# Index scores rectified in place in PSUM and begun four steps sooner, low weights of a joint computed inside the pipeline of heads, two waits made finer

## The reference

```python
s = einsum('bqhd,bkd->bqhk', qib, ki)                 # 8 index heads of width 32, one shared key
score = einsum('bqhk,bqh->bqk', relu(s), wb)           # rectified, weighted, summed over heads
score = where(causal, score, -inf); _, sel = top_k(score, 128)
c_sel = c[sel]; logits = einsum('bqhd,bqkd->bqhk', qb, c_sel) * ATTN_SCALE
p = softmax(logits); out = einsum('bqhk,bqkd->bqhd', p, c_sel)
m = g0 * y_a + g1 * (out @ w_b) + g2 * y_c;  h = h + m @ w_o      # then a gated FFN
```

## Time and profile before

| | |
|---|---|
| median of three runs | 2055.36 us |
| the profiled execution: own time / span of the profile | 2055.58 us / 2053.4 us |
| PE matmuls busy | 2026.3 us, 99% of the span, 9561 records |
| PE weight loads busy (beside the matmuls) | 1675.5 us, 82% |
| DVE / ACT / POOL busy | 892.2 us (43%) / 720.7 us (35%) / 1020.1 us (50%) |
| chain that ended last | PE 94%, DVE 3%, POOL, ACT and issue 1% each |
| DMA | 188.20 MB, mean 92 GB/s |

### The profile page before, as it was taken

One profiled execution on the slowest core, in us unless ns is written; L12 is line 12 of the kernel. 1 busy time (PEld: TensorE's weight loads), 2 busy tenths in 40 slices (PEclk: granted clock), 3 DMA queues, 4 the chain that ended last, 5 costly groups with the idle time before them and its releaser, 6 DMA issues.

```text
span 2053.4 us, 26660 instructions
## 1 busy us (share of the span) xinstructions
PE 2026.3 (99%) x9561; PEld 1675.5 (82%) x9561; DVE 892.2 (43%) x1366; ACT 720.7 (35%) x990; POOL 1020.1 (50%) x783
## 2 busy tenths in 40 slices
PE   8999999999999999999999999999999999999999
PEld 7798887678888888888888887888877888888887
DVE  6778644534333322153334103568854533332124
ACT  6413224434322223232222223567543422222232
POOL 5345442135555554555555444666644555554543
PEclk9999999999999999999999999999999999999999
DMA  4232322013333332333333232332222333332232
GB/s 159 63 107 83 103 83 81 21 65 99 103 102 85 99 97 93 97 102 95 88 102 97 92 97 83 94 107 58 90 65 86 99 102 102 86 98 98 92 108 82
DMA packets 254152, 188.20 MB, mean 92 GB/s; under 512 B 7552, under 2 KB 249728, under 8 KB 254080
## 3 DMA queue, kind: packets, MB, share of 16 engines
q1 hardware_dynamic: 253392, 186.93, 30.4%
q10 hardware_dynamic: 688, 0.31, 0.1%
HBM read 180.93 MB, written 2.10 MB: 89 GB/s over the span
## 4 chain that ended last, share of the span: by engine, by line
PE 94%; DVE 3%; POOL 1%; issue 1%; ACT 1%; DMA 0%; SPq 0%; DVEq 0%; ACTq 0%; POOLq 0%
PE ps L600 29%; PE ps L602 29%; PE ps L601 28%; DVE sc L1430 1%; PE ps L823 1%; PE ps L808 1%; PE ps L966 1%; PE ps L889 1%; PE ps L891 1%; PE ps L890 1%; DVE ssum L1558 0%; POOL wlo L552 0%; PE ps L822 0%; PE ps L954 0%; PE ps L816 0%
## 5 line engine op out<-in xcount | busy, mean ns | idle before, releaser
L497 POOL TENSOR_TENSOR wlo<-raw,whi 128x512 fp32r<-128x512 f32 (+1 forms) x640 | 871.0, 1392 | 913.4 <-ACT whi L1030 913.1
L600 PE MATMUL ps<-xh,whi 128*128 128x512 f32 (+2 forms) x1912 | 732.9, 383 | 8.9 <-DVE xl L1430 7.4
L602 PE MATMUL ps<-xh,wlo 128*128 128x512 f32 (+2 forms) x1912 | 722.5, 378 | 0.0
L601 PE MATMUL ps<-xl,whi 128*128 128x512 f32 (+2 forms) x1912 | 722.2, 378 | 0.0
L1030 ACT ACTIVATE whi<-raw 128x2048 fp32r<-128x2048 f32 (+1 forms) x159 | 297.5, 1871 | 796.1 <-PE ps L602 792.9
L600 PEld LDWEIGHTS ps<-xh,whi 128*128 128x128 f32 (+1 forms) x1912 | 358.4, 187 | 77.5 <-issue 9.8
L602 PEld LDWEIGHTS ps<-xh,wlo 128*128 128x128 f32 (+1 forms) x1912 | 358.1, 187 | 68.0
L601 PEld LDWEIGHTS ps<-xl,whi 128*128 128x128 f32 (+1 forms) x1912 | 358.7, 188 | 64.9 <-issue 2.5
L1484 DVE TENSOR_TENSOR tmp<-ps,rs 128x512 f32<-128x512 f32 x148 | 102.1, 692 | 325.9 <-PE ps L602 308.6
L600 PE MATMUL ps<-fh,whi 128*128 128x512 f32 x528 | 205.4, 389 | 0.0
L602 PE MATMUL ps<-fh,wlo 128*128 128x512 f32 x528 | 205.4, 389 | 0.0
(11 more groups left out here) (290 smaller groups left out, 2208.1 us busy)
## 6 DMA issues: line engine op xcount, KB each, us to landing
raw<-in_w_in SPq DMA_DIRECT2D x90, 512.0 KB, 4.6
raw<-in_w_gate_up SPq DMA_DIRECT2D x44, 512.0 KB, 4.7
raw<-in_ffn_w_gate SPq DMA_DIRECT2D x44, 512.0 KB, 3.9
raw<-in_ffn_w_up SPq DMA_DIRECT2D x44, 512.0 KB, 5.1
raw<-in_ffn_w_down SPq DMA_DIRECT2D x32, 512.0 KB, 4.0
raw<-in_w_down SPq DMA_DIRECT2D x16, 512.0 KB, 3.9
raw<-in_ffn_w_down SPq DMA_DIRECT2D x16, 384.0 KB, 3.5
raw<-in_w_b SPq DMA_DIRECT2D x8, 512.0 KB, 3.9
```

Source lines behind the costliest of these rows:

```text
L497: ins = pool.tensor_tensor(wlo[:, c % 2, cs], raw[:, c % 2, cs], whi[:, c % 2, cs].bitcast(F32), ALU.subtract)
L600: pe.matmul(o, w_of(whi), xhi, start=first, stop=False)
L601: pe.matmul(o, w_of(whi), xlo, start=False, stop=False)
L602: return pe.matmul(o, w_of(wlo), xhi, start=False, stop=last)
```

## The change

1. **Scores.** ACT rectifies a score in place in its PSUM bank; DVE accumulates from PSUM; the SBUF buffers `rl` are gone. A bank is free again only after the accumulation (`score_acc` in place of `relu_done`). Score 0 moves from step (1, 0) to step (0, 4) of `C_Q+1`; `score_window` gives DVE's share per tile.
2. **Stack.** ACT writes `qst` and `kst` rows once (four copies and one); SP copies them to the repeated rows with two DMAs (32 partitions each: 66 KB for `kst`, 512 KB for `qst`), placed before the load of chunk `C_Q+3`. PE's first score waits for these copies.
3. **ACT's high weights** of `C_Q+3` and `C_U` are done in quarters between the rectifications.
4. **DVE.** The eight search steps among the scores go (the search runs on in the later slices), and `cT` is computed after the last query tile.
5. **Norm sums** are called after step (0, 5) of `C_QI`.
6. **Joint.** POOL computes `wlo` of `C_MX` in parts during the last chunk of the pipeline, ahead of `pair_low(7)`; `C_MX+1` follows outside of the loop.
7. **Waits.** `C_WB` waits for `y_split` k + 1 at each step k; `acc_free` 2*C_WB stays. `C_PP` waits for `acc_free` 2*C_PP - 2.

```diff
+SCORE_LEAD = 4
+def score_window(j, t):
+    first = DK * (2 * j + t) - SCORE_LEAD
+    return range(max(first, 0), min(first + DK, len(SCORES)))
...
-        rl = at("rl", 18224, [P, 2, TM])
... SyncE, in the loop of square(c0 + j, ...)
+                    if c0 + j == C_Q + 3:
+                        sp.wait_ge(ks_hi, 1)
+                        sp.dma_start(kst[D_IDX:2 * D_IDX, :].bitcast(F32), kst[0:D_IDX, :].bitcast(F32)).then_inc(ks_dup, 16)
+                        sp.wait_ge(qst_hi, 4)
+                        sp.dma_start(qst[2 * D_IDX:3 * D_IDX, :, :].bitcast(F32),
+                                     qst[0:D_IDX, :, :].bitcast(F32)).then_inc(qst_dup, 16)
... GpSimd
-                    if third < 3 and j < 13:
+                    if third < 3:
                         low_of_part(c, third)
             pair_low(7)
-            run(C_MX, C_D[2], 2)
+            low(C_MX + 1)
+            run(C_MX + 2, C_D[2], 2)
... TensorE
-                            pe.wait_ge(m_split, ready + k + 1)
+                            pe.wait_ge(ready[0], ready[1] + k + 1)
-            chunk(C_QI, xh, xl, steps=lambda t, k: norm_sums(0, C_QI) if (t, k) == (0, 3) else None)
+            chunk(C_QI, xh, xl, steps=lambda t, k: norm_sums(0, C_QI) if (t, k) == (0, 5) else None)
             def score(n):
                 if n >= 4:
-                    pe.wait_ge(relu_done, n - 3)
+                    pe.wait_ge(score_acc, n - 3)
...
-                    n = DK * (2 * j + t - 1) + k
+                    n = DK * (2 * j + t) + k - SCORE_LEAD
                     if n == 0:
-                        pe.wait_ge(qst_hi, 8)
+                        pe.wait_ge(qst_dup, 16)
                         pe.wait_ge(qst_lo, 4)
-                        pe.wait_ge(ks_hi, 2)
+                        pe.wait_ge(ks_dup, 16)
...
-            pe.wait_ge(att["dsa"]["y_split"], HEADS)
             pe.wait_ge(acc_free, 2 * C_WB)
             with pe.Fori(0, 2) as i:
                 for j in range(2):
-                    chunk(C_WB + j, ath, atl, 2, i)
+                    chunk(C_WB + j, ath, atl, 2, i, ready=(att["dsa"]["y_split"], 0))
...
-            pe.wait_ge(acc_free, 2 * C_PP)
+            pe.wait_ge(acc_free, 2 * C_PP - 2)
... ScalarE
-            for z in range(2):
-                act.activation(kst[D_IDX * z:D_IDX * z + D_IDX, :], kw[0:D_IDX, :], ACT.Copy).then_inc(ks_hi, 1)
+            act.activation(kst[0:D_IDX, :], kw[0:D_IDX, :], ACT.Copy).then_inc(ks_hi, 1)
...
-            for part in (0, 2):
-                for g in range(4):
+            for g in range(4):
...
+            def high_quarter(c, z):
+                if z == 0:
+                    act.wait_ge(raw_in[c % 2], raw_level(c, 0, None))
+                    act.wait_ge(tile_done, 2 * (c - 1))
+                cs = slice(CH // 4 * z, CH // 4 * z + CH // 4)
+                ins = act.activation(whi[:, c % 2, cs], raw[:, c % 2, cs], ACT.Copy)
+                if z == 3:
+                    ins.then_inc(w_hi, 1)
             for n, (q, h, k0, k1) in enumerate(SCORES):
+                s = ps[:, score_bank(n), 0:k1 - k0]
                 act.wait_ge(s_ready, n + 1)
-                if n >= 2:
-                    act.wait_ge(score_acc, n - 1)
-                act.activation(rl[:, n % 2, 0:k1 - k0], ps[:, score_bank(n), 0:k1 - k0], ACT.Relu).then_inc(relu_done, 1)
-                if n % (2 * DK) == DK - 1:
-                    high(C_Q + 3 + n // (2 * DK))
+                act.activation(s, s, ACT.Relu).then_inc(relu_done, 1)
+                j, z = divmod(n + SCORE_LEAD + 1 - 2 * DK, 2 * DK)
+                if j >= 0 and z < 4:
+                    high_quarter(C_Q + 3 + j, z)
+            high(C_U + 1)
... VectorE
-                r, a = rl[:, n % 2, 0:k1 - k0], sc[:, q, k0:k1]
+                r, a = ps[:, score_bank(n), 0:k1 - k0], sc[:, q, k0:k1]
...
-                    for n in range(max(DK * (2 * j + t - 1), 0), DK * (2 * j + t)):
+                    for n in score_window(j, t):
                         add_score(n)
                     query(C_Q + 1 + j, t)
-                    if j == 0 and t == 0:
-                        dve.wait_ge(crt_done, 1)
-                        link(dve.reciprocal(rc[:], rt[:]))
-                        stt(cT[:], cl[:], vec[:, V_KV:V_KV + 1], rc[:], ALU.mult, ALU.mult).then_inc(c_done, 1)
-                    if j:
-                        some_search(2)
+            dve.wait_ge(crt_done, 1)
+            link(dve.reciprocal(rc[:], rt[:]))
+            stt(cT[:], cl[:], vec[:, V_KV:V_KV + 1], rc[:], ALU.mult, ALU.mult).then_inc(c_done, 1)
```

More of the change, by code:

```diff
@@ L258, in build @@
         sc_zero = sem("sc_zero")
+        ks_dup, qst_dup = sem("ks_dup"), sem("qst_dup")
         s_ready, relu_done, score_acc = sem("s_ready"), sem("relu_done"), sem("score_acc")
@@ L740, in turn_latents @@
             def turn_latents():
-                pe.wait_ge(relu_done, len(SCORES))
+                pe.wait_ge(score_acc, len(SCORES))
                 pe.wait_ge(c_done, 1)
@@ L746, in turn_latents @@
                 pe.transpose(ps[0:META, 7, 0:P], cT[:, 0:META], ident[:]).then_inc(c_turned, 1)
-            pe.wait_ge(relu_done, len(SCORES) - 2)
+            pe.wait_ge(score_acc, len(SCORES) - 2)
             chunk(C_U, xh, xl, full=(True, True), between=turn_latents)
@@ L846, in _ @@
                 for j in range(2):
-                    chunk(C_WB + j, ath, atl, 2, i)
+                    chunk(C_WB + j, ath, atl, 2, i, ready=(att["dsa"]["y_split"], 0))
             with pe.Fori(0, 2) as i:
                 for j in range(2):
-                    chunk(C_O + j, mh, ml, 2, i, ready=0)
+                    chunk(C_O + j, mh, ml, 2, i, ready=(m_split, 0))
             ffn(0, 1, 1)
@@ L995, in _ @@
                 for j in range(2):
-                    chunk(C_O2 + j, m2h, m2l, 2, i, ready=DK)
+                    chunk(C_O2 + j, m2h, m2l, 2, i, ready=(m_split, DK))
             ffn(2, 4, 4)
@@ L1130, in _ @@
             act.activation(qih[:], qiT[:], ACT.Copy).then_inc(qi_hi, 1)
-            for part in (0, 2):
-                for g in range(4):
-                    act.activation(qst[D_IDX * part:D_IDX * part + D_IDX, g:HEADS:4, :],
-                                   qiT[D_IDX * g:D_IDX * g + D_IDX, :, :], ACT.Copy).then_inc(qst_hi, 1)
+            for g in range(4):
+                act.activation(qst[0:D_IDX, g:HEADS:4, :],
+                               qiT[D_IDX * g:D_IDX * g + D_IDX, :, :], ACT.Copy).then_inc(qst_hi, 1)
             act.wait_ge(css_done, 1)
```

## The result

The changed kernel takes 2037.13 us (median of 4 runs, 2036.84 to 2038.86), the kernel before, timed beside it, 2055.37 (2055.08 to 2055.56): ratio 0.9913, 95% interval 0.9896 to 0.9930. Forecast were 2037.7 us and 2035.5 to 2041.5. The profiled execution took 2037.16 us.

The account below looks back on a forecast made before the run. PE bounds the kernel (matmuls fill 99%), so only delayed PE starts count. 0.9 + 7.6 + 8.2 + 1.0 = 17.7 us off the profiled 2055.58 gave 2037.9, predicted as 2037.7 us; range 2035.5 to 2041.5 for 8 in 10.

Parts of the forecast that it names:

- Norm sums, -0.9: Norm sums in `C_QI`: called later, PE's wait for DVE's last `ssum` goes, 0.9 us less, with 0.06 left for operand change.
- Scores, -7.6: Score stage, `C_Q+1` to `C_U`: at most 7.8 us to be had, 0.2 given back for small waits, 7.6 us less.
- floor of 38.9: Score stage: PE's own work of 32.64 us plus 6.24 for the scores, reached if nothing stalls, against 46.70 before.
- 0.7 was the bound: Score stage: a DVE accumulation from PSUM takes at most 0.7 us for 400 columns and less for the rest.
- 4.6 taken: Copies before the first score: the 512 KB DMA lands in 4.6 us, so no wait; the other end costs 1.3 us.
- slower rival: Score stage: accumulations from PSUM stay at 1.41 us, 40 of them make it 60.1 us, about 2059 in all; chance 2%.
- all 40 `hT` instructions: Score stage evidence: same kind of PSUM-sourced DVE instruction, 512 columns, mean 691 ns over 40, POOL said to work beside all.
- Its rival: `cT` after the last query tile: slowed by POOL, 7.0 us against 6.1, late by about 1 us, 2038.7; chance 7%.
- Joint, -8.2: Entry of the joint: the 5.40 us gap on POOL and the 2.87 us of low clock go together, 8.2 us less.
- Last projection, -1.0: `C_PP`: the wait names an earlier tile, PE's 1.03 us of standing goes and the end moves with it, 1.0 us less.
- `C_WB`, 0: `C_WB`: the removed wait part, `atl`, was over before `gb`, which stays, so nothing is gained.
- Sum 17.7: Whole kernel: norm sums 0.9, scores 7.6, joint 8.2 and last projection 1.0 add up to 17.7 us saved.

Follow-up runs that it names:

- 9: The changed kernel with the norm sums two steps earlier, at (0, 3), where the kernel before has them: 2038.22 us, ratio 0.9918.
- 3: The kernel before with only ACT's in-place rectification and DVE's accumulation from PSUM; score start, search and `cT` stay where they were: 2050.30 us, ratio 0.9975.
- 5: The kernel before with POOL's low-weight work beside the scores cut to a 64th, the rest left out of the computation: 2049.58 us, ratio 0.9974.
- 7: The changed kernel with the eight search steps put back among the scores, two after each tile of `C_Q+2` and `C_Q+3`: 2038.61 us, ratio 0.9922.
- 8: The changed kernel with the reciprocal and `cT` put back behind the first query tile, among the first scores: 2039.16 us, ratio 0.9924.
- 4: The changed kernel with the two SBUF `rl` buffers back, so DVE accumulates from SBUF; the waits for the last accumulations stay: 2038.62 us, ratio 0.9918.
- 6: The changed kernel with score 0 four steps later, as in the kernel before, and ACT's quarters of `C_U` behind the scores: 2038.52 us, ratio 0.9918.
- Experiment 1: The kernel before with 22 idle matmuls on PE ahead of its wait at the joint, filling the gap: 2053.11 us, ratio 0.9990.
- 11: The changed kernel with `C_WB`'s wait for its accumulation banks split by tile, the second bank awaited between the tiles: 2035.81 us, ratio 0.9906.
- 2: The kernel before with only the joint's part of the change, POOL computing its low weights in parts during the last chunk: 2047.43 us, ratio 0.9960.

## Why the prediction was right

Step by step, against the ledger:

- *Norm sums, -0.9.* 1.06 measured, and given back in full when undone (9). I had kept 0.06 back for the change of operand; nothing was lost there, and behind no gap the sums themselves took 0.1 less (0.69 us to the next matmul instead of 0.80).
- *Scores, -7.6.* 8.01. The floor of 38.9 was meant as the best case and the stage came to 38.69, so the 0.2 for small waits was not needed. The terms behind it: accumulations of 0.36 to 0.63 us (0.7 was the bound); in-place rectification of 0.28 to 0.49 by width; the DMA of 512 KB landed in 4.3 us (4.6 taken), at about 46.4, with score 0 at 50.14. The mechanism is shown by 3 and 5: the 1.41 us came with GpSimd's work and left with it (at most 0.64), and it left also when one operand came from PSUM though GpSimd worked on (0.50). That is the rule of the Trainium skill ("SBUF — State Buffer", SBUF's two separate sides) that the prediction weighed, and both experiments agree with it.
- *What it read wrongly there.* It says that the 1.41 us paced the stage, and prices its slower rival with 40 of them. Seven of the 40 were slow; the others took 0.36 to 0.64 us, and experiments 7 and 8 show waits that the search and `cT` cause without any slow one. The gain did not hang on it, since it was taken from the floor, but the rival's 2059 us did. It also took all 40 `hT` instructions as having POOL beside them; 20 overlap one of POOL's and took 692 ns against 690 for the others, so the argument from them holds.
- *`cT`.* Its rival was priced at 7.0 us against 6.1 and given 7%. From the query tile's start it took 5.16 us (85.63 to 90.79), and PE asked after 5.64 (91.27). The direction was right: 1.07 us instead of 0.77 with POOL beside it, but no POOL instruction had to be waited for in full. With 0.48 us to spare it was the closest call of the forecast, and here some luck was in it: the prediction had no way to tell how the two engines' instructions would meet. `cT` took 1.07 or 1.08 us in all five profiles with this order, but 1.53 and 1.72 in experiments 4 and 6; with 1.72 it would have ended at 91.44, too late. In experiments 4, 6 and 7 it is late.
- *Joint, -8.2.* 5.33 for the gap and 2.87 for the clock, 8.20. Experiment 1 separates them: clock without gap. The rule of the Trainium skill ("TensorE: Matmul & The Clock Gate", "What's actually happening") gives both together, as measured.
- *Last projection, -1.0.* 1.06.
- *`C_WB`, 0.* 0.08 over the whole stretch to it. The reason holds, and 11 shows the wait that was left.
- *Sum 17.7.* 18.34 at `C_PP`, 18.24 in the medians. The 0.64 between is 0.41 at the scores, 0.16 at the norm sums, 0.08 and 0.06 at `C_WB` and `C_PP`, less the 0.07 by which this execution started later.

What the prediction had not seen is in the experiments: it treated the moves of start, search and `cT` as costing or keeping something each and the PSUM operand as the cause of the gain. Experiment 4 says that without this operand the rest would have brought 7.3 of the 8.0 us in the stage (and lost 1.0 of it at `cT`). The sum was right since it went by a floor that the stage reached, not since the share of each part was known.

## What to carry to other kernels

Where PE is full at 99%, keep a ledger of its starts at the borders of the stages, and price a standstill with what its clock does behind it: idle matmuls in the gap save only the second part (2.75 us of 8.2 here), no gap saves both. Parts of a change that relieve the same engine don't add up: work the sum out from the floor of the bound engine, and test each part with the others in place before crediting it. When a semaphore counts several things, ask which of them the very next instruction needs: at `C_PP` the finer wait brought 1.1 us, at `C_WB` the one by tile 1.3, and the one on `y_split`, which was not the late part, nothing.

## What the runs showed of the hardware

- PE's clock fell to its lower level (0.50, 1.2 GHz) behind starts 5.6 us apart in all three profiles with the joint's gap left empty, but the slow stretch cost 2.9 us in two of them and 1.5 in a third, so that the price of such a gap is not a fixed one. It may differ between executions of one kernel as well: of 42 of the kernel before, timed in the experiments, five have a mean granted clock of 0.999 and 2054.09 to 2054.73 us, the others 0.998 and 2054.41 to 2057.25. No profile shows this.
- It fell also behind starts 2.2 us apart at the entry of `C_QI` (clock 0.72 over 24 to 30 us, experiments 2 and 6), and not behind 1.5 to 1.9 us there (the changed kernel, experiments 4, 5 and 11). In experiments 1, 2, 6, 7 and 9 one execution each has a mean clock of 0.999 and not 1.000, and each time it is the slowest.
- Beside GpSimd an accumulation of 272 columns from SBUF took 1.33 to 1.36 us instead of 0.50, but `cT` (528 columns, its inputs in SBUF too) took 0.82, 1.07, 1.53 and 1.72 us (experiment 7, the changed kernel, experiments 4 and 6) and 0.77 without: how much such an instruction is stretched depends on how the two engines' instructions meet. The loss goes both ways: beside these accumulations GpSimd's `wlo` instructions took 1.46 to 1.49 us instead of 1.29.
- The reciprocal of 528 columns, with one input in SBUF, took 3.44 us beside GpSimd (the changed kernel) as without (experiment 5).
- Rectifying 272 columns in place in PSUM took ACT 0.38 us, no more than to SBUF (0.40).
